# A two-layer hybrid attention block: the exponent's bias formed by ScalarE in layer 0 and by POOL in layer 1, with layer 1's bias tables spread over steps

## The chip, the core and the metric

One core of a Trainium2 chip runs the whole program. The metric is the device time of one execution in microseconds. The engines are TensorE (PE), VectorE (DVE), ScalarE (ACT), GpSimd (POOL) and SyncE (SP), which here only issues transfers; each works through its own queue in order, and they meet through semaphores. "L1536" is line 1536 of the kernel before.

## The reference

Two layers of a transformer block over 512 latent tokens and 256 context tokens of width 1024, one sample. Each layer: modulated RMS norm, one input projection, three groups of attention heads, output projection, gated residual, and a SwiGLU feed-forward part with its own norm and residual. Only layer 0 updates the context tokens.

```python
h = modulate(rms_norm(x, g_attn), sh_a, sc_a)
q_w, k_w, v_w, q_n, k_n, v_n, q_g, k_g, v_g = split_mixer_inputs(h @ w_in, qk_g)
o = concatenate([window_attention(...),         # A: 6 heads, window of 3 blocks, sink logits
                 neighbourhood_attention(...),  # B: 4 heads, 8 x 16 neighbourhood, position bias
                 global_block_attention(...)])  # C: 6 heads, all keys
x = x + ga_a * (o @ w_out)
x = x + ga_f * swiglu(modulate(rms_norm(x, g_ffn), sh_f, sc_f), w_gate, w_up, w_down)
# context queries (layer 0 only) attend to the 256 context keys alone
```

Every softmax is over local keys and the 256 context keys together. In each, the kernel computes the row maximum m of the scores, then exp(s * score - s * m + SHIFT), where s undoes a scale by a power of two that the queries and keys carry; so the bias of the exponent is (-s) * m + SHIFT.

## The kernel before

Attention is cut into steps (`STEPS`, index g): one head and 128 queries each. Layer 0 has 96: 24 of group A, 12 of context queries of A, 24 of group C, 20 of context queries of C and B, 16 of group B. Layer 1 has 64: 24 A, 24 C, 16 B. A step has 256 to 768 keys (768 in group C, 512 in B, 512 or 640 in A, 256 for context queries). Four steps make a group of one head (or two heads of context queries). The steps run from 234 to 446 us in layer 0 and from 1275 to 1425 us in layer 1; the rest of the time is projections and feed-forward, in which PE is the busy engine.

For step g, in order of dependence:

- `score(g)` on PE: scores into one of two PSUM buffers `acc[g % 2]` (L895, L896, masks L899). It waits for the exponent of step g-2.
- `top_of(g)` on DVE: in group B the bias table is added to the local scores (L1533), then `reduce_max` gives the row maximum into `stat` row 0 (L1536, semaphore `top`).
- `minus_top(g)` on DVE: the bias of the exponent, 128x1, into `stat` row 1 (L1543, semaphore `neg_top`).
- `softmax(g)` on ACT: the exponent of the scores with that bias and the sum of a row (L1199, an activation and the read of the accumulator; semaphore `exps`).
- `turn(g)` on PE: the probabilities are transposed, 128 columns at a time, into one of three banks (L912).
- `turned_high(g)` on ACT: the bank rounded to 16 bits, in pieces of up to 512 columns (L1221); `turned_low(g)` on DVE: the difference to it (L1550).
- `weigh(g)` on PE: both halves times the values (L927, L929) into `small`; after every fourth step `sum_outputs` on DVE adds the halves (L1558, L1562), and `take_output` on POOL divides by the row sums (L630, L632). `weigh` of the next group's first step waits for the sum.

Each engine has its order written out. DVE in iteration g: the sum of outputs if g is a multiple of four, `top_of(g)`, `minus_top(g)`, `turned_low(g-2)`. ACT: `turned_high(g-2)`, `softmax(g)`. PE: `score(g)`, `turn(g-2)`, `weigh(g-4)`, and in layer 0, every second or third step, a unit of modulation (`modulation`, L696 and L705), whose result ACT takes (L1210, L1213). The last three of the input projection's units (13 to 15) are finished within the first ten steps: norm (`norm_tile`, L1453 and L1464, which wait for a transfer of inverse norms), rounding (`round_high` L1157 on ACT, `round_low` L1491 on DVE) and eight transfers each, issued by SP.

POOL's main work is `split`: each tile of weights that a transfer has brought is rounded (L566) and its remainder formed (L569), two buffers deep. Its queue in the attention stage of layer 1 is: `split_next(0)` and `split_next(1)` for the first two tiles of the output weights, then for k in 0 to 15 `take_output(k)`, and after k = 8 to 11 one head's bias table (`bias_tables`: one scaling L606 and three additions L610). In layer 0 the splits of modulation weights lie between the outputs, and the tables follow k = 16 to 19. The remaining splits of output weights follow the last output.

## Time and profile before

| | |
|---|---|
| median of 3 runs (lowest, highest) | 1866.49 us (1864.91, 1866.91) |
| the profiled execution | 1864.14 us, its span 1862.3 us |
| PE, PEld busy | 1745.9 us (94%), 1475.2 us (79%) |
| DVE, ACT, POOL busy | 914.6 us (49%), 484.3 us (26%), 862.5 us (46%) |
| subtraction of the maximum, L1543 | 160 times, 34.3 us in all, 214 ns each |
| maximum, L1536 | 160 times, 117.4 us in all |
| exponent, L1199 | 160 times, 130.9 us, and 31.1 us of accumulator reads |
| idle time of ACT that L1543 ended | 55.0 us, 89 times |
| chain that ended last, share by engine | PE 79%, DVE 12%, issue 3%, DMA 2%, POOL 2%, ACT 2% |

The busy times are of the whole span, three quarters of which aren't attention. Within the two attention stages the shares are others, and they have to be read window by window. A row of the timeline gives the start in us, the length in us, engine, line, operation, output and input, and in brackets the idle time before it with what ended it. Instructions that don't depend on each other overlap a little at their ends: a row's length includes the time in which its result is written, while the next may have started.

### The profile page before, as it was taken

To read this page: it belongs to the slowest core of one execution; us is meant where nothing else is said; L and a number is where in the kernel's file an instruction comes from. 1 tells how busy PE (TensorE), PEld (TensorE's weight loads), DVE (VectorE), ACT (ScalarE), POOL (GpSimd) and SP (SyncE) were. 2 spreads that over 40 slices of the span, in tenths; PEclk is the share of its full clock that TensorE was granted. 3 is DMA by queue.
4 is the path that set the end of the run, shared out by engine and by line. 5 is a ranking of instruction groups with operands and counts; after the bars stand their busy time and mean duration, and the time that the engine had idled before them with its cause. 6 is when DMAs were issued, how large, how long until landed. Compare 5 with 4: busy or idle time off the path is not lost.

```text
span 1862.3 us, 30083 instructions
## 1 busy us (share of the span) xinstructions
PE 1745.9 (94%) x11175; PEld 1475.2 (79%) x11175; DVE 914.6 (49%) x1615; ACT 484.3 (26%) x984; POOL 862.5 (46%) x671
## 2 busy tenths in 40 slices
PE   5899979987989999999999998998887999999998
PEld 3588868976878888888888887887776778888886
DVE  2525478886355461255315455456996633123122
ACT  2212267775120100000000012224775121010010
POOL 0234337884324544444444453542021566666664
PEclk9999989999999999999999998998998999999999
DMA  8234444432114432334223322443200323333332
GB/s 293 46 91 115 114 120 120 132 92 57 57 38 132 124 102 68 102 114 122 80 80 112 116 65 46 113 110 100 50 2 1 91 79 94 98 92 100 92 94 96
DMA packets 316392, 174.42 MB, mean 94 GB/s; under 512 B 87550, under 2 KB 307598, under 8 KB 316302
## 3 DMA queue, kind: packets, MB, share of 16 engines
q1 hardware_dynamic: 288608, 148.54, 28.7%
q10 hardware_dynamic: 27694, 24.66, 4.2%
q8 instruction: 58, 0.95, 0.2%
q14 instruction: 32, 0.26, 0.0%
HBM read 159.04 MB, written 2.83 MB: 87 GB/s over the span
## 4 chain that ended last, share of the span: by engine, by line
PE 79%; DVE 12%; issue 3%; DMA 2%; POOL 2%; ACT 2%; SPq 1%; ACTq 0%; DVEq 0%; POOLq 0%
PE acc L746 66%; DVE prob_t L1550 3%; DVE stat L1536 3%; PE side L705 1%; PE mod_ps L818 1%; DVE o_sum L1562 1%; PE side L912 1%; PE small L988 1%; POOL split_w L569 1%; PE small L927 1%; PE acc L895 1%; PE acc L896 1%; PE mod_ps L716 1%; DVE stat L1543 1%; PE small L838 1%
## 5 line engine op out<-in xcount | busy, mean ns | idle before, releaser
L746 PE MATMUL acc<-act,split_w 128*128 128x512 f32 x5088 | 1006.3, 358 | 22.3 <-DVE act L1377 16.3
L746 PEld LDWEIGHTS acc<-act,split_w 128*128 128x128 f32 x5088 | 835.5, 190 | 171.6 <-issue 15.9
L569 POOL TENSOR_TENSOR split_w<-raw_w,split_w 128x1024 fp32r<-128x1024 f32 (+1 forms) x220 | 519.7, 2362 | 18.4
L566 POOL TENSOR_SCALAR split_w<-raw_w 128x1024 fp32r<-128x1024 f32 (+1 forms) x220 | 228.8, 1040 | 315.0 <-PE acc L746 205.2
L746 PE MATMUL acc<-hidden,split_w 128*128 128x512 f32 (+1 forms) x1584 | 308.8, 357 | 0.2 <-DVE hidden L1619 0.2
L746 PEld LDWEIGHTS acc<-hidden,split_w 128*128 128x128 f32 x1584 | 261.7, 188 | 46.0 <-DVE hidden L1619 0.6
L565 POOL TENSOR_TENSOR turnstile<-ones 128x1 f32<-128x1 f32 x136 | 53.6, 394 | 454.9 <-PE acc L746 454.9
L1617 DVE TENSOR_TENSOR prod<-acc,silu_g 128x768 f32<-128x768 f32 (+1 forms) x44 | 36.3, 824 | 331.1 <-PE acc L746 331.1
L1397 DVE SCALAR_TENSOR_TENSOR x_t<-acc,mod,x_t 128x512 f32 (+1 forms) x96 | 60.6, 659 | 258.4 <-PE acc L746 258.4
L1261 ACT ACTIVATE silu_g<-acc 128x768 f32<-128x768 f32 (+1 forms) x44 | 31.1, 706 | 455.3 <-PE acc L746 455.3
L1199 ACT ACTIVATE prob<-acc,stat,score_scale 128x768 f32<-128x768 f32 (+5 forms) x160 | 130.9, 818 | 57.1 <-DVE stat L1543 55.0
L1536 DVE TENSOR_REDUCE stat<-acc 128x1 f32<-128x768 f32 (+5 forms) x160 | 117.4, 734 | 22.8 <-PE acc L896 13.0
L1619 DVE TENSOR_TENSOR hidden<-prod,hidden 128x512 f32 (+2 forms) x44 | 105.3, 2392 | 45.7 <-ACT hidden L1269 45.7
L1642 DVE SCALAR_TENSOR_TENSOR mod_acc<-mod_chunk,silu_c,mod_acc 128x256 f32<-128x256 f32 x308 | 123.7, 473 | 0.0
L1269 ACT ACTIVATE hidden<-prod 128x512 f32 (+2 forms) x44 | 32.6, 740 | 314.9 <-DVE prod L1617 314.9
L927 PE MATMUL small<-v,prob_t 128*128 128x128 f16 x696 | 83.0, 223 | 26.6 <-DVE o_sum L1562 25.0
L895 PE MATMUL acc<-ks,qs 128*128 128x256 f16 (+1 forms) x384 | 94.8, 276 | 12.6 <-ACT prob L1199 12.1
L896 PE MATMUL acc<-ks,qs 128*128 128x256 f16 (+1 forms) x384 | 91.7, 274 | 0.0
L927 PEld LDWEIGHTS small<-v,prob_t 128*128 128x128 f16 x696 | 64.8, 100 | 33.2 <-DVE prob_t L1550 32.2
L630 POOL TENSOR_TENSOR o<-o_sum,stat 128x256 f32<-128x256 f32 x32 | 19.6, 612 | 146.7 <-DVE o_sum L1562 117.2
L912 PE MATMUL side<-ident,prob 128*128 128x128 f32 x470 | 79.2, 284 | 8.8 <-DVE prob_t L1550 8.4
L1550 DVE TENSOR_TENSOR prob_t<-side,prob_t 128x512 f16<-128x512 f32 (+2 forms) x154 | 84.2, 557 | 4.2 <-ACT prob_t L1221 2.5
(164 smaller groups left out, 1568.2 us busy)
## 6 DMA issues: line engine op xcount, KB each, us to landing
raw_w<-in_w_gate SPq DMA_DIRECT2D x44, 512.0 KB, 3.9
raw_w<-in_w_up SPq DMA_DIRECT2D x44, 512.0 KB, 3.8
mod_chunk<-in_w_mod ACTq DMA_DIRECT2D x22, 1024.0 KB, 5.3
raw_w<-in_w_mod SPq DMA_DIRECT2D x36, 512.0 KB, 3.9
raw_w<-in_w_in SPq DMA_DIRECT2D x64, 256.0 KB, 3.7
raw_w<-in_w_down SPq DMA_DIRECT2D x32, 512.0 KB, 4.0
mod_start<-in_w_mod SPq DMA_DIRECT2D x4, 2048.0 KB, 12.6
ks<-q_split SPq DMA_DIRECT2D x64, 96.0 KB, 2.2
```

The lines of the kernel that those rows point to most:

```text
L566: pool.tensor_scalar(split_w[slot][:, 0, 0:n, :], raw_w[slot][:, 0:n, :], 1.0, 0.0, ALU.mult, ALU.add).then_inc(hi_w, 1)
L569: pool.tensor_tensor(split_w[slot][:, 1, 0:n, :], raw_w[slot][:, 0:n, :], split_w[slot][:, 0, 0:n, :].bitcast(F32), ALU.subtract).then_inc ...
L746: mm = pe.matmul(acc[slot][:, a:b], split_w[slot][:, part == 2, k, :], moving[:, part == 1, k, a:b], start=(k == 0 and part == 0), stop=(k ...
L895: pe.matmul(out_, q, ks[:, s["k"], 0, k0:k0 + size], start=True, stop=False)
L896: mm = pe.matmul(out_, q, ks[:, s["k"], 1, k0:k0 + size], start=False, stop=not masks)
L912: mm = pe.transpose(turned_at[BANK_AT["p", c] % 3][:, t - a:t - a + P], prob[g % 3][:, 1 + t:1 + t + P], ident[:, :])
L927: pe.matmul(small[:, at_:at_ + 128], prob_t[g % 4][:, 0, P * t:P * t + P], v[:, 2 * vc:2 * vc + 128], start=(t == 0), stop=False)
L1199: sc.activation(prob[g % 3][:, 1 - s["sink"]:1 + n], src, ACT.Exp, bias=stat[:, 1, i:i + 1], scale=score_scale[:, 0, gi:gi + 1], accum_out ...
L1536: ve.reduce_max(stat[:, 0, i:i + 1], src, AX_X).then_inc(top, 1)
L1550: ve.tensor_tensor(prob_t[g % 4][:, 1, a:b], turned_at[BANK_AT["p", c] % 3][:, 0:b - a], prob_t[g % 4][:, 0, a:b], ALU.subtract).then_inc( ...
L1619: ve.tensor_tensor(hidden[:, 1, bass.ds(f, 1), 0:w].rearrange("p a t -> p (a t)"), prod[0][:, 0:w], hidden[:, 0, bass.ds(f, 1), 0:w].rearr ...
L1642: i = ve.scalar_tensor_tensor(**kw, in1=mod_acc[:, b, :], op0=ALU.mult, op1=ALU.add)
```

## The change

`minus_top` is removed from DVE. In layer 0, ACT forms the bias itself: at the start of `softmax(g)` it waits for the maximum, runs an Identity activation of 128x1 with a scale from `score_scale` and a bias from the new constant `exp_shift`, waits for its own result and then runs the exponent. In layer 1, POOL does it with the same `tensor_scalar` as DVE did. POOL's queue in layer 1 becomes a loop over steps: the subtraction of step i; from i = 11 every fourth step the output of group (i - 11) / 4; and in steps 30 to 45 one operation of the bias tables each (scaling, or one of three additions), where before a table's four came together. The two splits of output weights stay ahead of that loop. POOL's order in layer 0 is unchanged.

```diff
+        exp_shift = place("exp_shift", [P, 1], F32)
...
+            pool.memset(exp_shift[:, :], SHIFT).then_inc(filled, 1)
...
-                def bias_tables(h):
-                    if l == 0 and h == 0:
-                        pool.wait_ge(consts_in, N_CONST * 16)
-                    if h == 0:
+                def bias_tables(h, i):
+
+                    if h == 0 and i == 0:
+                        if l == 0:
+                            pool.wait_ge(consts_in, N_CONST * 16)
                         pool.wait_ge(wide_in, 16 * 4 * ROWS * (l + 1))
                         pool.wait_ge(unit_done, u_in(l) + 16)
...
+                def minus_top(g):
+
+                    s, i = STEPS[g], g - LAYER_STEPS[l][0]
+                    gi = 3 * l + "ABC".index(s["group"])
+                    pool.wait_ge(top, g + 1)
+                    pool.tensor_scalar(stat[:, 1, i:i + 1], stat[:, 0, i:i + 1], score_scale[:, 2, gi:gi + 1], SHIFT, ALU.mult,
+                                       ALU.add).then_inc(neg_top, 1)
...
-                for k in range(N_GROUPS[l]):
+                for k in range(N_GROUPS[l] if l == 0 else 0):
...
-                    if (16 if l == 0 else 8) <= k < (20 if l == 0 else 12):
-                        bias_tables(k - (16 if l == 0 else 8))
+                    if 16 <= k < 20:
+                        for i in range(4):
+                            bias_tables(k - 16, i)
+                for i in range(4 * N_GROUPS[l] + 8 if l else 0):
+                    if i < 4 * N_GROUPS[l]:
+                        minus_top(LAYER_STEPS[l][0] + i)
+                    if i >= 11 and i % 4 == 3:
+                        take_output((i - 11) // 4)
+                    if 30 <= i < 46:
+                        bias_tables((i - 30) // 4, (i - 30) % 4)
...
                 def softmax(g):
                     s = STEPS[g]
                     i, n, gi = g - LAYER_STEPS[l][0], s["n"], 3 * l + "ABC".index(s["group"])
+                    if l == 0:
+                        if g == 0:
+                            sc.wait_ge(filled, 3)
+                        sc.wait_ge(top, g + 1)
+                        sc.activation(stat[:, 1, i:i + 1], stat[:, 0, i:i + 1], ACT.Identity, bias=exp_shift[:, 0:1],
+                                      scale=score_scale[:, 2, gi:gi + 1]).then_inc(neg_top, 1)
                     sc.wait_ge(neg_top, g + 1)
...
-                def minus_top(g):
-
-                    s, i = STEPS[g], g - LAYER_STEPS[l][0]
-                    gi = 3 * l + "ABC".index(s["group"])
-                    ve.wait_ge(top, g + 1)
-                    ve.tensor_scalar(stat[:, 1, i:i + 1], stat[:, 0, i:i + 1], score_scale[:, 2, gi:gi + 1], SHIFT, ALU.mult,
-                                     ALU.add).then_inc(neg_top, 1)
-
...
                         top_of(g)
-                        minus_top(g)
```

## Rows read from the trace of the kernel before

**Rows 1.** Busy time by windows: us, PE, PEld, DVE, ACT, POOL, PEclk, DMA

```profile
330.00:390.00 60.00, 58.07 (x769) 54.29 (x768) 49.38 (x107) 46.75 (x120) 48.63 (x33) 1.00 0.44 127
...
1345.00:1384.00 39.00, 36.17 (x426) 30.43 (x422) 38.36 (x81) 32.79 (x71) 7.82 (x12) 1.00 0.01 2
```

**Rows 2.** Timeline of DVE, layer 1, group C: one group of four steps

```profile
1358.11 0.95 DVE L1536 TENSOR_REDUCE stat<-acc 128x1 f32<-128x768 f32 x1
...
1359.23 1.01 DVE L1550 TENSOR_TENSOR prob_t<-side,prob_t 128x512 f16<-128x512 f32 x2
1360.16 0.95 DVE L1536 TENSOR_REDUCE stat<-acc 128x1 f32<-128x768 f32 x1
...
1366.36 0.66 DVE L1562 TENSOR_REDUCE o_sum<-small 128x256 f32<-128x512 f32 x1
1366.94 0.95 DVE L1536 TENSOR_REDUCE stat<-acc 128x1 f32<-128x768 f32 x1
```

**Rows 3.** Timeline of ACT, layer 1, group C, the same steps

```profile
1361.39 0.99 ACT L1199 ACTIVATE prob<-acc,stat,score_scale 128x768 f32<-128x768 f32 x1 [0.20 <-DVE stat L1543]
...
1362.38 0.58 ACT L1221 ACTIVATE prob_t<-side 128x512 f16<-128x512 f32 x1
```

**Rows 4.** POOL: an output in the timeline, and two lines' lengths (min/median/max)

```profile
1367.10 0.61 POOL L630 TENSOR_TENSOR o<-o_sum,stat 128x256 f32<-128x256 f32 x1 [8.21 <-DVE o_sum L1562]
...
L565 POOL TENSOR_TENSOR turnstile<-ones x136: 192/194/2693, 520.9 to 1844.0; 128x1 f32<-128x1 f32 x136
...
L606 POOL TENSOR_SCALAR wide<-wide,score_scale x8: 579/586/589, 399.4 to 1394.3; 128x384 f32<-128x384 f32 x8
```

**Rows 5.** Timeline of DVE and ACT, layer 1, group B

```profile
1402.58 0.69 DVE L1536 TENSOR_REDUCE stat<-acc 128x1 f32<-128x512 f32 x1
...
1404.49 0.69 DVE L1536 TENSOR_REDUCE stat<-acc 128x1 f32<-128x512 f32 x1
...
1410.89 0.69 DVE L1536 TENSOR_REDUCE stat<-acc 128x1 f32<-128x512 f32 x1
...
1405.47 0.78 ACT L1199 ACTIVATE prob<-acc,stat,score_scale 128x512 f32<-128x512 f32 x1 [0.55 <-DVE stat L1543]
```

**Rows 6.** Timeline of DVE, layer 1, group A: the maxima of steps 13 and 16

```profile
1311.08 0.83 DVE L1536 TENSOR_REDUCE stat<-acc 128x1 f32<-128x641 f32 x1
...
1316.91 0.69 DVE L1536 TENSOR_REDUCE stat<-acc 128x1 f32<-128x513 f32 x1
```

**Rows 7.** Timeline of POOL, ACT and DVE at the start of attention in layer 1

```profile
1281.81 2.35 POOL L569 TENSOR_TENSOR split_w<-raw_w,split_w 128x1024 fp32r<-128x1024 f32 x1
...
1279.18 0.78 ACT L1199 ACTIVATE prob<-acc,stat,score_scale 128x513 f32<-128x513 f32 x1
...
1281.61 0.83 DVE L1536 TENSOR_REDUCE stat<-acc 128x1 f32<-128x641 f32 x1 [0.78 <-PE acc L899]
...
1284.05 0.48 DVE L1453 SCALAR_TENSOR_TENSOR q_raw<-raw_q,vecs,root 128x256 f32<-128x256 f32 x1 [1.37 <-DMA root<-inv_rows]
...
1285.91 0.69 DVE L1550 TENSOR_TENSOR prob_t<-side,prob_t 128x512 f16<-128x512 f32 x1
```

**Rows 8.** ACT's Identity of two columns, lengths (min/median/max)

```profile
L1210 ACT ACTIVATE mod<-side,vecs x26: 250/262/278, 263.8 to 432.9; 128x2 f32<-128x2 f32 x26
```

**Rows 9.** Timeline of ACT and DVE, layer 0, context queries: one group

```profile
394.67 0.57 ACT L1199 ACTIVATE prob<-acc,stat,score_scale 128x256 f32<-128x256 f32 x1
...
396.67 0.57 ACT L1199 ACTIVATE prob<-acc,stat,score_scale 128x256 f32<-128x256 f32 x1
...
399.33 0.57 ACT L1199 ACTIVATE prob<-acc,stat,score_scale 128x256 f32<-128x256 f32 x1 [0.71 <-DVE stat L1543]
...
398.63 0.41 DVE L1536 TENSOR_REDUCE stat<-acc 128x1 f32<-128x256 f32 x1
```

**Rows 10.** Timeline of POOL at the start of layer 1's attention

```profile
1275.09 1.04 POOL L566 TENSOR_SCALAR split_w<-raw_w 128x1024 fp32r<-128x1024 f32 x1 [11.16 <-DMA raw_w<-in_w_out]
...
1279.92 1.80 POOL L566 TENSOR_SCALAR split_w<-raw_w 128x1024 fp32r<-128x1024 f32 x1 [1.36 <-DMA raw_w<-in_w_out]
```

## What the change is predicted to do

> **What bounds the kernel now.** I read the windows first, then the timeline inside them, then the chain of waits in order of time. The change touches only the two attention stages (234 to 446 us in layer 0, 1275 to 1425 us in layer 1). In layer 1, DVE is busy 38.36 of 39.00 us while PE has 36.17, ACT 32.79 and POOL 7.82; in the corresponding part of layer 0, where PE also computes modulations, it is PE that is full (58.07 of 60.00 us) and DVE has 49.38 [rows 1]. So one operation removed from DVE can shorten layer 1 and the parts of layer 0 where PE is not the last; where PE is, it buys nothing.
>
> The timeline of DVE shows what the subtraction costs there. In group C a step is 2.04 us (maximum to maximum). The maximum that starts at 1358.11 ends at 1359.06, and the first difference of the turned probabilities starts at 1359.23; the subtraction lies in that gap of 0.17 [rows 2]. The next maximum begins at 1360.16, 0.08 before the two differences end (1360.24): independent instructions of DVE overlap by that much. Without the subtraction the difference could start at 1358.98, so the slot is worth 0.25 us; I take 0.23, since the overlap behind a reduction is not shown. Four steps and one sum of outputs make a group of 1366.94 - 1358.11 = 8.83 us [rows 2].
>
> **What takes the subtraction's place in layer 1.** Now the way from the end of the maximum to the exponent is x = 0.28 us (maximum of 1360.16, which ends at 1361.11, to the exponent at 1361.39) [rows 2, 3]. With POOL there are two handoffs. DVE to POOL is 0.08 us: the sum of outputs ends at 1367.02, POOL starts at 1367.10 [rows 2, 4]. To ACT I take 0.04. The subtraction itself, 128x1 on POOL, isn't shown: its nearest rows are the turnstile's product, also 128x1, 0.194 us in the median, and the scaling of 384 columns with a pointer, 0.586 [rows 4]. It is nearest to the first; with a little for the pointer I take 0.23, and x = 0.35. The ends are x = 0.31 and 0.71.
>
> This matters because the next limit is near. ACT turns the older tile high only after the exponent of the step before, and DVE's difference waits for that. From one maximum to the one two steps on: 0.95 (maximum) + x + 0.99 (exponent 1361.39 to turned-high 1362.38) + 0.61 (turned-high and handoff) + 0.93 (two differences, 1359.23 to 1360.16) = 3.48 + x [rows 2, 3]. Twice that with the sum's 0.66 is a group: 7.62 + 2x. Now it is 8.18, hidden under DVE's 8.83. Afterwards DVE alone would need 8.83 - 4 x 0.23 = 7.91, and the loop, 8.32, is the later one. **Group C gains 0.51 us, not 0.92; six groups, 3.1 us.**
>
> Group B has a step of 1.91 and a group of 8.31 us (1402.58 to 1410.89) [rows 5]. Its loop is 0.69 (maximum) + x + 0.78 (exponent) + 0.61 + 1.05 (what a step of 1.91 leaves beside the maximum and the gap of 0.17: the difference and the addition of the bias) = 3.13 + x; the group 6.92 + 2x = 7.62, DVE alone 7.39 [rows 5, 2]. **Gain 0.69, four groups, 2.8 us.**
>
> Group A already waits on the way round through PE: from the maximum at 1311.08, over its exponent, the scores two steps later, the turn and both halves of the split, to the maximum at 1316.91, three steps; only one step of four is DVE alone [rows 6]. So a group gains 0.23 and pays x - 0.28 = 0.07: 0.16, for three settled groups 0.5 us.
>
> **The start of layer 1 pays.** POOL's queue has the splits of the first two tiles of the output weights ahead of the first subtraction, and the second of them ends at 1284.16. The exponent of step 0 started at 1279.18 [rows 7]. Behind the waiting POOL instruction stand all further subtractions; behind them ACT's exponents, PE's scores of step 2 (they reuse the bank) and then DVE. Step by step: subtraction 0 ends at 1284.35, exponent 0 with its accumulator read at 1285.3; the scores of step 2 and their handoff take 1.5 us, as now (exponent and read end at 1280.1, maximum 2 starts at 1281.61), so it starts near 1286.8; then come the two operations of unit 13 (from 1284.05 now, where they waited for a transfer), and the first difference falls at about 1289.45 instead of 1285.91 [rows 7]. That is 3.5 us late, not 5.2, because 1.6 us of it were spent waiting for the transfer. The slots removed up to step 11 give back little over 0.4 of it, since split and exponent are then waited for: **+3.1 us**. The transfer of unit 15, 2 us later, still lands before it is read.
>
> The bias tables in layer 1 become one operation a step (0.59 or 0.74 us) in steps 30 to 45. Before, four in a row would have held up a subtraction for 2.8 us; now at most 0.74 + 0.61 (the output) lie between two that are 1.9 us apart, so I cost them at nothing. If that cover failed, 0.1 us a step, 1.6 in all. The outputs are taken three steps later, well before their buffer is wanted two groups on. The loads of the bias lie ahead of step 30 in the timeline, so POOL doesn't wait for them there.
>
> Layer 1: 3.1 - 0.5 - 3.1 - 2.8 = -3.3; as a function of the handoff, 25x - 12.0 us.
>
> **Layer 0, with ACT.** An Identity with a bias takes 0.262 us [rows 8]; from the maximum's end to the exponent y = 0.03 + 0.25 + 0.04 = 0.32. Exponent and Identity exist side by side there already without table loads between them. Four parts:
> - Context queries (32 steps, 8 groups). From exponent to exponent: two steps of 2.00 together (394.67 to 396.67), then 1.96 to the next group's maximum and 0.70 to its exponent, 4.66 in all (to 399.33) [rows 9]. ACT's step becomes 0.56 (exponent, read) + 0.27 + 0.29 (Identity, which the exponent must wait for) = 1.12 instead of 1.00: 2.24 + 1.96 + 0.73 = 4.93. **+0.27 a group, +2.2 us.** The bounds: 0 and 0.29 in every one of 32 steps, 9 us, which would need ACT to be last everywhere; it isn't at the sum.
> - Group C (24 steps): PE is full there [rows 1]. ACT's step would be 0.99 + 0.86 (two turned-high) - 0.1 (overlap) + 0.29 = 2.04, under the 2.6 us at which PE runs on average with a modulation in every second step: +0.3, from 0 to 2.
> - Group B: as in layer 1 with y: 7.56 against 8.31, 0.75; in one of four groups a modulation on PE is last: -2.3.
> - Start: DVE is on the chain up to the load that follows unit 15; five slots of 0.2, less 0.28 for the Identity before the first exponent: -0.7. Group A behind it waits for weights and PE: 0.
>
> Layer 0: -0.5. **Sum: -3.8 us.** It is made against the profiled execution (span 1862.3, 1864.14 with what lies around it); the median of the runs is 1866.49, 2.35 above that, and the difference is applied to it: 1862.7.
>
> **Port.** At 1279.92 POOL's scaling of 1024 columns took 1.80 us, beside DVE's difference of unit 12, which has both inputs in SBUF; at 1275.09, alone, the same form took 1.04 [rows 10]. The Trainium skill (SBUF — State Buffer, two separate sides) says the two engines share one port pair as an exclusive lock, for DVE instructions with two SBUF inputs, and that the loser is blocked for the whole instruction. By that rule a form of 1.04 is held for 0.76 us here; the trace agrees. The maxima and differences of the steady part read PSUM, and POOL's product at 1367.10, beside a maximum, took its usual 0.61 [rows 4]. Only seven operations of units 12 to 15, in steps 1 to 9, remain, and most of what they delay waits for PE anyway.
>
> **Rivals.**
> 1. DVE alone sets the pace (a slot saved is a slot won, the loop is shorter than I add up). C 5.5, B 3.7, A 2.8 won in layer 1, +3.1 at the start, -0.5 in layer 0: -9.4 us, 1857.1. For it: DVE 98% busy [rows 1]. Against it: the loop adds up from rows and is over DVE's need. Chance 0.15.
> 2. The handoff over POOL is long. From x = 0.48 layer 1 gains nothing, from x = 0.65 (0.53 us on POOL) the kernel is slower by over 3.7; at the upper end, 0.71, it is +5.7 in layer 1, +5.2 in all: 1871.7. For it: the 384 columns' 0.586; against it: the median of the 128x1 product. Chance 0.12.
> 3. The lock of the port holds the subtractions of steps 2 to 9 and each hold reaches the end: 4 x 0.76 beside the differences and 3 x 1.86 beside the norms (1284.05 to 1285.91) [rows 7] = 8.6 us on top of the forecast, 1871.3. Chance 0.07; against it, ACT and PE have 0.5 to 2 us of slack in six of the seven places.
> 4. No change: x near 0.5 (0.38 on POOL), or ACT in layer 0 costs 3 us more: 1866. Chance 0.24.
> The forecast has 0.42.
>
> **How the numbers follow.** A kernel of this time is told from no change at about 0.2%, 3.7 us. The forecast sits on that bound, so half of it counts as faster (0.21) and half as same; with rival 1, and a little of rival 4, faster is 0.37; same 0.44; rivals 2 and 3, slower, 0.19. The range from 1858 to 1870.5 takes in the forecast and rival 4, and of the others the milder halves.
>
> **What would show it.** Right: POOL's new row near 0.23 us, 64 times; group C of layer 1 near 8.3 us, B near 7.6, DVE idle behind ACT's turned-high; the first exponent of layer 1 at about 1284 (less what layer 0 won); a group of context steps near 4.9. Wrong: groups of C at 7.9 (rival 1) or 8.8 and more (2); POOL rows of 1 us in steps 2 to 9 with idle DVE behind them (3); a table load between Identity and exponent in each step would end the whole sum.

## The result, and the profile after

The changed kernel takes 1870.87 us in the median of 10 runs (1867.29 to 1873.18), the kernel before, run in turns with it, 1866.33 (1862.42 to 1870.43): ratio 1.0026, 95% interval 1.0015 to 1.0037. It is slower by 0.26%, where 0.2% gain was forecast. The profiled execution took 1871.29 us, its span is 1869.5, 7.2 us over that of before.

The two new kinds of instruction first: all subtractions on POOL (L624) and all Identities on ScalarE (L1219) of the changed kernel. Columns: count, length in ns (min/median/max), first and last start, shapes.

```profile
L624 POOL TENSOR_SCALAR stat<-stat,score_scale x64: 267/267/1322, 1288.1 to 1417.9; 128x1 f32<-128x1 f32 x64
...
L1219 ACT ACTIVATE stat<-stat,exp_shift,score_scale x96: 371/386/394, 242.3 to 450.0; 128x1 f32<-128x1 f32 x96
```

POOL's takes 0.267 us, near the 0.23 assumed; ScalarE's takes 0.386, where the row of an Identity that was used as its price has 0.262 [rows 8]. The windows of the changed kernel that answer to [rows 1] (us, then busy PE, PEld, DVE, ACT, POOL, granted clock, share and GB/s of the transfers):

```profile
330.00:390.00 60.00, 58.75 (x767) 54.87 (x767) 46.02 (x79) 53.12 (x141) 49.11 (x33) 1.00 0.44 126
1345.00:1384.00 39.00, 35.77 (x449) 32.08 (x448) 37.12 (x65) 33.60 (x76) 18.34 (x38) 1.00 0.01 2
```

In layer 1 DVE is no longer full (37.12 of 39.00 against 38.36) although more steps fit in; in layer 0 ScalarE has become much busier (53.12 of 60 against 46.75).

To see where time went, I compared the starts of all 160 maxima, before and after. d is after minus before:

| place | before, us | d |
|---|---|---|
| layer 0, step 0 | 234.37 | +3.82 |
| step 24, context queries of A begin | 301.92 | +3.50 |
| step 36, group C begins | 318.93 | +6.42 |
| step 60, context queries of C and B begin | 382.32 | +6.98 |
| step 80, group B begins | 410.45 | +8.83 |
| step 95, the last | 441.41 | +7.88 |
| layer 1, step 0 | 1275.74 | +4.89 |
| step 12 | 1309.23 | +6.04 |
| step 24, group C begins | 1332.07 | +5.36 |
| step 48, group B begins | 1385.06 | +3.13 |
| the last step, 63 | 1416.88 | +0.20 |
| feed-forward of layer 1, the long chain begins | 1499.80 | +2.05 |
| the end of the span | 1862.3 | +7.2 |

Layer 0's attention loses 4.1 us (3.82 to 7.88) and layer 1's gains 4.7 (4.89 to 0.20). But 7.0 us appear behind both, in stages whose instructions the change doesn't touch, 5.2 of them from the start of the long chain on, and 3.0 are won between the two attention stages. The first 3.8 stand there before the change acts; the runs below show such an offset between -3.9 and +3.8 at step 0, one per execution, and I leave it out of everything. The late loss is in one row of the chain of work that ended last (start, length, line, number of matmuls), of before and of after:

```profile
1499.80 318.90 PE acc L746 x1392
```

```profile
1501.85 323.74 PE acc L766 x1392
```

The same 1392 matmuls of 512 columns, back to back, at a granted clock of 1.00 in both: 229.1 ns each before, 232.6 ns after. In layer 0's feed-forward the opposite holds: 480 matmuls take 84.88 us before and 84.38 after. Something in the change altered the pace of TensorE where no instruction of it was changed. The one thing in the diff that reaches so far is the new tile: `exp_shift` takes 64 bytes in the layout, and every tile placed behind it (the activations `act`, `hidden`, the queries, keys and values) starts 64 bytes later.

### The profile page after: what moved, and what is told of

Same layout as the page of the kernel before. It is cut to its first block, busy times and chain, and to the rows that moved or that the text cites. A ratio compares the mean times of both kernels' runs of the same rounds, so it can differ in the third digit from the quotient of the medians.

```text
span 1869.5 us, 30085 instructions
## 1 busy us (share of the span) xinstructions
PE 1749.2 (94%) x11175; PEld 1475.4 (79%) x11175; DVE 887.9 (47%) x1455; ACT 512.1 (27%) x1080; POOL 884.3 (47%) x736
## 4 chain that ended last, share of the span: by engine, by line
PE 79%; DVE 7%; issue 4%; ACT 4%; POOL 2%; DMA 2%; SPq 1%; ACTq 0%; DVEq 0%; POOLq 0%
PE acc L766 65%; ACT prob_t L1247 1%; PE side L932 1%; PE mod_ps L838 1%; DVE prob_t L1568 1%; DVE stat L1562 1%; PE small L947 1%; PE acc L915 1%; POOL split_w L571 1%; PE side L725 1%; PE acc L916 1%; ACT prob L1225 1%; DVE o_sum L1580 1%; PE small L1008 1%; PE mod_ps L736 1%
## 5 line engine op out<-in xcount | busy, mean ns | idle before, releaser
L949 PE MATMUL small<-v,prob_t 128*128 128x64 f16 x696 | 77.9, 195 | 0.0
```

## The experiments

Theory P: the loss is that place effect, ScalarE's work in layer 0 costs less than 2 us, and POOL's part in layer 1 does what was predicted. Rival Q: the attention stages alone account for the loss, and the pace of the matmuls is chance.

### 1. Only the room: e1_room_only

```diff
         eps = place("eps", [P, 1], F32)
+        room = place("room", [P, 1], F32)
```

> The kernel before, with one unused tile of 64 bytes placed behind eps, where the change places its new tile exp_shift; every tile behind it (act, hidden, the queries, keys and values among them) moves by 64 bytes, and no instruction is added, removed or reordered. Theory P (place): the change's own loss lies in TensorE's streams outside attention, whose matmuls of 512 columns took 232.6 ns with the change against 229.1 before (1392 of them, +4.8 us, and +0.7 in two shorter chains), those of 384 columns 176.7 against 177.5 (-3 us in all); then this kernel is 2 to 5 us slower than before, about +0.2%, and shows 232 to 233 ns in the long chain of layer 1. Theory Q (attention): the loss lies in layer 0's attention, which the profiled pair shows 4.1 us longer, and the rate of the matmuls is a matter of the execution: then this kernel is within 1 us of before and shows 229 ns, or either rate at random.

Measured: 1867.04 us (12 runs) against 1864.69, ratio 1.0018, interval 1.0008 to 1.0027; the long chain takes 323.75 us, 232.6 ns a matmul, and the 480 of layer 0 84.38 us, what the changed kernel shows, to 0.01 us. By the ratio an unused tile of 64 bytes costs 3.4 us, with an interval from 1.5 to 5.0; the medians lie 2.4 us apart, and the trace of this kernel is 3.1 us longer than that of before, counted from the first maximum. On the place, P holds.

### 2. The whole change, nothing moved: e2_same_addresses

```diff
+        eps_at = at[0]
         eps = place("eps", [P, 1], F32)
-        exp_shift = place("exp_shift", [P, 1], F32)
+        exp_shift = place("exp_shift", [P, 1], F32, eps_at + 32)
```

> The whole change, but exp_shift placed in the unused 32 bytes behind eps, so that no other tile moves. Theory P: the long chain of layer 1 goes back to 229 ns a matmul and the kernel is 2 to 5 us faster than the changed kernel, 1866 to 1869, at most 0.1% from before. Theory Q: as the changed kernel, +0.2 to +0.3% against before.

Measured: 1866.79 us against 1864.69, ratio 1.0007 (0.9996 to 1.0017); the chain is back at 318.90 us. The edit itself isn't told from no change. The two ratios differ by 0.19%, with an uncertainty of some 0.15%: most of the 0.26% came from where a constant was put.

### 3. POOL in layer 1 alone: e3_pool_only

The diff of the change without exp_shift and without ScalarE's part; in layer 0 VectorE subtracts:

```diff
                         top_of(g)
+                        if l == 0:
+                            minus_top(g)
```

> POOL subtracts in layer 1, with the bias tables spread over steps; layer 0 as before on VectorE, no exp_shift, all addresses as before. The prediction's terms for layer 1 sum to -3.3 us; the profiled pair shows -4.7 for that stage (start +1.15, groups of A -0.22, of C -0.39, of B -0.55 to -0.7 each). Theories P and Q: 3 to 5 us faster than before, ratio 0.997 to 0.9985. If instead the gain of a shorter attention stage is given back behind it (the same total at another place), the ratio is 0.9995 to 1.0005 and the stretch from the last step to the end is longer by as much.

Measured: 1861.31 us (12 runs) against 1864.69, ratio 0.9985 (0.9976 to 0.9995). Layer 0's maxima lie at -0.18 to -0.33 us against before at every step, so nothing disturbs the reading. In layer 1 d goes from +0.32 at step 0 to +2.32 at step 12 (start: +2.0), to +1.62 at step 24 (A: -0.7), to -0.68 at step 48 (C: -2.3), to -3.63 at the last (B: -2.95): -3.95 in all.

### 4. ScalarE in layer 0 alone: e4_act_only

```diff
+                    if l == 0:
+                        if g == 0:
+                            sc.wait_ge(filled, 3)
+                        sc.wait_ge(top, g + 1)
+                        sc.activation(stat[:, 1, i:i + 1], stat[:, 0, i:i + 1], ACT.Identity, bias=exp_shift[:, 0:1],
+                                      scale=score_scale[:, 2, gi:gi + 1]).then_inc(neg_top, 1)
                     sc.wait_ge(neg_top, g + 1)
...
-                        minus_top(g)
+                        if l:
+                            minus_top(g)
```

> ScalarE forms the bias in layer 0, layer 1 as before, exp_shift in the gap behind eps, all addresses as before. The prediction's terms for layer 0 sum to -0.5 us (context steps +2.2, C +0.3, B -2.3, start -0.7). Theory P: within 2 us of before (the 4.1 of the profiled pair hold a stretch of 7 us at a granted clock of 0.6 to 0.7, at 315 to 322 us, that is not the change's). Theory Q: 3 to 6 us slower, ratio 1.0015 to 1.003, with the context groups at 5.2 us and more where 4.93 was forecast, and group B at 8.1 where 7.56 was.

Measured: 1869.84 us against 1864.69, ratio 1.0027 (1.0019 to 1.0036). Here P's figure (within 2 us) is missed and Q's is hit, in the context groups and group B too (5.30 and 8.06 us): ScalarE's part costs 5 us by itself. Both effects are real: place +0.18%, ScalarE +0.27%, POOL -0.15% add to +0.30% beside the 0.26% of the whole change; each of the three is known to about 0.1%, so that they agree this closely is in part luck. The profiled execution, whose trace is read here, was with 1873.79 us the second slowest of 11. d in layer 0: step 0 +2.23, step 24 +0.41, step 36 +3.31, step 60 +3.84, step 80 +7.77, step 95 +6.80.

What a context step has become shows in ScalarE's timeline of this kernel (start, length, line, operation, in brackets the idle time before it):

```profile
400.40 0.56 ACT L1208 ACTIVATE prob<-acc,stat,score_scale 128x256 f32<-128x256 f32 x1
400.86 0.19 ACT L1208 ACTIVATION_READ_ACCUMULATOR prob<-acc,stat,score_scale 128x1 f32 x1
400.95 0.37 ACT L1230 ACTIVATE prob_t<-side 128x256 f16<-128x256 f32 x1
...
401.22 0.38 ACT L1202 ACTIVATE stat<-stat,exp_shift,score_scale 128x1 f32<-128x1 f32 x1
401.63 0.57 ACT L1208 ACTIVATE prob<-acc,stat,score_scale 128x256 f32<-128x256 f32 x1
```

No idle time: ScalarE is full, and from exponent to exponent it is 1.23 us, where 1.12 was predicted and 1.00 was before [rows 9]. The Identity is followed by the exponent only at 401.63, 0.41 after its own start.

And a second thing, in the windows of e4_act_only:

```profile
310.00:325.00 15.00, 12.46 (x114) 10.56 (x113) 8.62 (x24) 11.76 (x38) 8.69 (x7) 0.77 0.33 89
...
410.00:420.00 10.00, 9.25 (x79) 8.01 (x80) 5.89 (x16) 6.71 (x21) 9.19 (x12) 0.66 0.28 80
```

The granted clock is 0.77 and 0.66 in these two, in or behind context queries: part of each was run at 1.2 GHz instead of 2.4. In the kernel before the first of them stands at 1.00:

```profile
310.00:325.00 15.00, 12.44 (x147) 10.87 (x145) 12.68 (x36) 11.32 (x34) 11.04 (x9) 1.00 0.29 79
```

Ahead of the second one TensorE had idled more, 6.34 us busy in 10 us against 7.53 before; experiment 9 has a trace that speaks against this as the whole cause. The changed kernel has the first fall as well (0.77) and not the second: its groups of context steps from step 76 to 80 take 6.19 us, those of e4_act_only 8.27. So one fall costs 2.1 us. e2_same_addresses, the whole change, has both falls (0.77, and 0.68 in the second window).

### 5. The context steps back on VectorE: e6_context_on_vector

```diff
-                    if l == 0:
+                    if l == 0 and s["local"]:
...
-                        if l:
+                        if l or not STEPS[g]["local"]:
                             minus_top(g)
```

(ScalarE's own steps count on a semaphore of their own.)

> ScalarE forms the bias in the local steps of layer 0 only; in its 32 context steps, and in layer 1, VectorE subtracts as before; a semaphore of its own orders ScalarE's part; addresses as before. Theory K (context steps): in e4_act_only ScalarE is full in them, a step takes 1.235 us instead of 1.00, and TensorE, which then idles, falls to half its clock at 315 and at 410 us; without them the granted clock stays at 1.00 there, the stage keeps the gains of groups A and B (-1.8 and -0.95 us) and the kernel is 1 to 3 us faster than before, ratio 0.9985 to 0.9995. Theory L (the drop of the clock is set off by group A's altered rhythm or by group C's): a stretch at 0.5 to 0.6 near 315 us remains, and the kernel is at least 1 us slower than before.

Measured: 1865.86 us (11 runs) against 1865.81, ratio 1.0001 (0.9992 to 1.0010). Neither theory's time came: K had 1 to 3 us less than before, L at least 1 us more. The clock, as K had it, stays at full speed in both places,

```profile
310.00:325.00 15.00, 12.44 (x147) 10.95 (x148) 11.65 (x36) 11.13 (x36) 10.14 (x9) 1.00 0.29 78
...
410.00:420.00 10.00, 8.47 (x96) 7.26 (x94) 9.17 (x23) 8.44 (x24) 9.75 (x11) 1.00 0.30 86
```

and the context groups are back at their old length (d is +2.05 at step 24 and +1.90 at step 36, +2.33 at step 64 and +2.32 at step 80). Against e4_act_only, 0.26% is won back: it is the context steps that cost ScalarE's part its time. But the kernel is not faster than before: its trace gains 0.9 us in layer 0, and group A, which gained 1.8 us in e4_act_only, gains 0.2 here. In e4_act_only and in the changed kernel the clock is full from 270 to 290 us; here, as in the kernel before, it is 0.91. Up to the end of group A ScalarE does the same in these two kernels, and yet one trace has this fall and the other hasn't. I can say where the falls stood, not what places them.

### 6. The cost of the Identity: e12_copy_without_shift

```diff
-                        sc.activation(stat[:, 1, i:i + 1], stat[:, 0, i:i + 1], ACT.Identity, bias=exp_shift[:, 0:1],
+                        sc.activation(stat[:, 1, i:i + 1], stat[:, 0, i:i + 1], ACT.Copy,
                                       scale=score_scale[:, 2, gi:gi + 1]).then_inc(neg_top, 1)
```

> e4_act_only with ScalarE's Identity replaced by a Copy that takes the scale from its tile and no bias: the constant SHIFT is left out of the exponent in layer 0 (it cancels in the quotient but for rounding). The Identity with two operands from tiles measured 0.386 us where the prediction took 0.262, the row of an Identity with one. If the second operand makes that difference, the Copy takes 0.25 to 0.27, a context step 1.11 us instead of 1.235, and groups of context steps fall from 5.1 to 5.3 us to the 4.9 that was predicted. If the length has another reason (one column, source in SBUF), it stays at 0.38 and nothing moves.

```profile
L1202 ACT ACTIVATE stat<-stat,score_scale x96: 278/295/302, 237.1 to 440.4; 128x1 f32<-128x1 f32 x96
```

0.295 us instead of 0.386, 0.091 less. The edit takes away the bias operand and also puts Copy for Identity, and no run separates the two; but [rows 8] is an Identity with one operand from a tile and takes 0.262, which points to the second operand. The Trainium skill (ScalarE: Activation LUTs, What ACT_TABLE_LOAD costs) gives about 93 ns for each operand of scale or bias that is a column of a tile, on top of 186 ns with immediates. An estimate by that page is 0.28 us with one and 0.37 with two; the trace agrees to 0.02 us.

Over 96 steps that takes 8.7 us of work from ScalarE. The one execution took 1864.24 us, 0.7 under the median of before on its chip, where e4_act_only was 5.2 over its own. From the first to the last maximum of layer 0 its trace is 6.1 us shorter than that of e4_act_only; the two falls of the clock, which it doesn't have, are 4.2 of them. d in layer 0: step 0 -0.17, step 24 -2.13, step 36 -1.78, step 60 -1.53, step 80 -0.33, step 95 -1.71. The two context groups from step 64 take 5.04 and 5.13 us instead of 5.30 and 5.33 (4.93 was predicted). The clock doesn't fall in either place (it does at the stage's end, from about 442 us on, without a visible price); from step 33 to step 40 d grows by 0.66 us, in the changed kernel by 2.72, which gives a fall's cost a second time, 2.1 us:

```profile
310.00:325.00 15.00, 12.69 (x145) 11.14 (x146) 10.49 (x24) 12.87 (x43) 10.56 (x9) 1.00 0.35 96
...
410.00:420.00 10.00, 9.53 (x119) 8.62 (x118) 9.33 (x19) 8.38 (x24) 9.75 (x10) 1.00 0.22 62
```

With the price that the prediction had assumed, nearly, layer 0 comes out at -1.5 us (-0.5 predicted). It is one execution; the steps inside it are as steady as in the others, the total is not to be read to a microsecond.

### 7. The start of layer 1: e5_vector_first_ten

```diff
-                    if i < 4 * N_GROUPS[l]:
+                    if 10 <= i < 4 * N_GROUPS[l]:
                         minus_top(LAYER_STEPS[l][0] + i)
...
-                        if l == 0:
+                        if l == 0 or g - g0 < 10:
                             minus_top(g)
```

> POOL in layer 1 alone, as in e3_pool_only, but the subtractions of the first ten steps stay on VectorE, so that none waits behind POOL's two splits and none meets VectorE's operations with two SBUF inputs. Theory S (the start costs what the prediction said): in e3_pool_only the maximum of step 12 is 2.0 us later against before than that of step 0; here it is level to within 0.4 us, and the kernel is 2 us faster than e3_pool_only: 5 to 6 us faster than before, ratio 0.9965 to 0.9975. Theory T (the lateness is made up later in any case, since what follows waits for the last units and weights): the time of e3_pool_only, ratio 0.998 to 0.999.

Measured: 1859.20 us (5 runs) against 1865.81, ratio 0.9965 (0.9951 to 0.9978). d goes from -2.21 at step 0 to -2.79 at step 12 and to -8.65 at the last step: 6.4 us won in the stage instead of 3.95. S holds: the first twelve steps win 0.6 where they lost 2.0, and what the start costs is not made up later.

### 8. What the place does: e7_room_128, e8_room_192, e11_weights_moved_too

As experiment 1, with 32 and 48 columns instead of one; in e11_weights_moved_too a tile of 64 bytes stands ahead of all tiles, the weights included. e7, e8 and e11 were run once each.

> The kernel before with 128 unused bytes behind eps. act, hidden and what follows then begin 64 bytes past a multiple of 256, where before they begin 192 past one and with 64 bytes added at one. Theory U (bits of the address above 64 bytes decide the rate): a third pair of rates, neither 229.1 and 176.8 ns nor 232.6 and 175.8, or the first pair again if only whether the address is a multiple of 128 counts. Theory V (any tile moved against the weights does it): the pair 232.6 and 175.8.

> As e7_room_128 with 192 bytes: act begins 128 past a multiple of 256. If only a multiple of 128 counts: 232.6 ns in layer 1 and 175.8 in layer 0, as with 64 bytes added. If 256 counts: 229 and another rate in layer 0.

> The kernel before with 64 unused bytes ahead of all tiles: the weights (split_w) move with act and hidden. If the address of the streamed tile alone decides, act begins at a multiple of 256 again and the rates are those of e1_room_only, 232.6 and 175.8 ns. If the distance between the weights and the streamed tile decides, it is unchanged and the rates are those of before, 229.1 and 176.8. Any other pair: both addresses take part.

| `act` moved against the weights | kernels | 1392 matmuls of layer 1, us | ns each | 480 of layer 0, us |
|---|---|---|---|---|
| 0 bytes | before, e2, e3, e4, e5, e6, e12 | 318.90 to 318.91 | 229.1 | 84.88 to 84.91 (e5: not in its chain) |
| 0, all moved by 64 | e11 | 318.90 | 229.1 | see below |
| 64 bytes | the change, e1 | 323.74, 323.75 | 232.6 | 84.38 |
| 128 bytes | e7 | 325.08 | 233.5 | 84.90 |
| 192 bytes | e8, e9, e10 | 315.82 to 315.84 | 226.9 | 83.31 (e8, e10) |

The rows of the chain for e8_room_192 and e11_weights_moved_too:

```profile
1491.26 315.82 PE acc L747 x1392
```

```profile
1498.30 318.90 PE acc L747 x1392
```

(e11's chain doesn't run through the 480 of layer 0; in the 220 us from 760 on it has 1272 matmuls, as the kernel before.) The pace of layer 1's chain repeats within a layout to 0.02 us in 320, over 14 executions on several chips, so it belongs to the layout, not to the execution. U holds for layer 1: there are four paces in steps of 64 bytes, and V falls. For 192 bytes 232.6 or 229 ns were expected, and neither came. e11 shows that the address of the streamed tile alone isn't what counts: with `split_w` moved along, the pace is the old one. The distance between tiles counts; that the weights are the other end of it is likely, but `x_t` and `raw_w` moved with them, so it is not shown. The Trainium skill (TensorE: Matmul & The Clock Gate, Step-by-step: what each phase is for) says that the streamed operand and the weights have read ports of their own, and that loading weights takes no bandwidth from a running matmul. No run here tests that statement; what they show is that the places of the tiles matter all the same, by up to 2.9% of a matmul.

e8_room_192 took 1852.24 us in its one run, 13.6 under the median of before; e7_room_128 took 1875.84.

### 9. The parts together: e10_change_and_room, e9_first_ten_and_room

The first is the whole change with 128 more bytes behind `exp_shift`; the second is experiment 7 with 192 bytes behind `eps`.

> The whole change with 128 unused bytes behind exp_shift, so that act, hidden and the rest lie 192 bytes further than before, as in e8_room_192, and not 64. Theory A: the change alone at unmoved addresses was +0.07%, and the place is worth what e8_room_192 shows: 1853 to 1856 us, ratio 0.993 to 0.995; the same edit, placed otherwise, is faster than the kernel before by ten times what its own work is worth. Against it: the rates go back to those of the changed kernel (232.6 and 175.8 ns), since exp_shift itself is what disturbs; then 1869 to 1872.

> e5_vector_first_ten (POOL subtracts from step 10 of layer 1 on, VectorE everywhere else) with 192 unused bytes behind eps. Theory A (the place of the tiles and the work in attention add up): e5_vector_first_ten was 6.5 us under before, and e8_room_192, one run, 13 to 14 us; the sum gives 1845 to 1847 us, ratio 0.989 to 0.990, with 227 ns in layer 1's long chain and 173.6 in layer 0's. Theory B (e8_room_192's single run was partly luck in the first 70 us, where executions differ by up to 8 us): the rates are the same, but the time is 1848 to 1853, ratio 0.991 to 0.993.

Measured: e10_change_and_room 1859.07 us (1846.38 to 1861.48, 7 runs) against 1864.95, ratio 0.9962 (0.9946 to 0.9979). The same edit that lost 0.26% wins 0.38% with one unused tile behind its constant. Both expected times, 1853 to 1856 and 1869 to 1872, were missed. e9_first_ten_and_room 1853.58 (1842.92 to 1856.79, 6 runs), ratio 0.9925 (0.9903 to 0.9947): it is 11 us under the kernel before, but less than the sum of its parts would give (theory B's ratio). Why shows in the windows of layer 0's feed-forward, first e8_room_192, then e9_first_ten_and_room:

```profile
760.00:980.00 220.00, 220.00 (x1296) 193.38 (x1295) 90.56 (x179) 14.13 (x17) 101.66 (x76) 1.00 0.34 104
```

```profile
760.00:980.00 220.00, 220.00 (x1270) 191.69 (x1270) 84.54 (x168) 14.10 (x17) 98.87 (x75) 1.00 0.34 103
```

1296 matmuls against 1270 in the same 220 us, from the same addresses, both at full clock and without a pause. From the last maximum of layer 0 to the first of layer 1, e9 is 8.0 us slower than e8. e10's profiled execution, the fastest of its seven, has 1297 matmuls there. So at this layout three traces show two paces in layer 0. That an execution gets one or the other fits the wide spread of these two kernels (15.1 and 13.9 us), but each was traced once, so it isn't shown. B had looked for the cause in the first 70 us; it is here. What chooses the level wasn't tried.

e10_change_and_room says something on the clock too. It is the whole change, with Identities of 0.386 us, and its clock stays full from 270 to 445 us. The 10 us ahead of the first fall, first e4_act_only, then e10:

```profile
304.00:314.00 10.00, 6.90 (x80) 5.62 (x80) 6.65 (x20) 8.98 (x29) 8.21 (x7) 1.00 0.44 117
```

```profile
304.00:314.00 10.00, 6.91 (x80) 5.62 (x80) 6.66 (x20) 8.99 (x29) 7.62 (x6) 1.00 0.44 117
...
310.00:325.00 15.00, 11.67 (x135) 10.14 (x134) 10.55 (x26) 12.99 (x41) 10.61 (x8) 1.00 0.33 87
...
410.00:420.00 10.00, 8.46 (x104) 7.49 (x101) 7.97 (x18) 8.81 (x27) 9.75 (x12) 1.00 0.35 101
```

TensorE and ScalarE did the same work at the same time, and the clock fell in one trace and not in the other. So neither the Identity's length nor TensorE's idle time decides alone whether a fall comes: the whole change has one fall in its own trace, two in e2_same_addresses and none here. The four traces with the full Identity in the context steps have five falls near 315 and 410 us; the ten others, e12_copy_without_shift among them, have none there. The comparison of e10 with the changed kernel gives a fall's price with the instructions unchanged: steps 32 to 36 take 5.60 us against 7.64.

## Why the prediction was wrong, step by step

**The step that was missing: where the new tile lies.** The prediction went through every instruction of the diff and gave its first line, the place of `exp_shift`, no term at all. It is worth +3.4 us (e1_room_only), two thirds of the loss, and lies almost wholly in stages that the prediction set aside as untouched. In the trace of e1_room_only it is +4.85 in the long chain, +0.4 behind it, +1.0 between layer 1's attention and the chain, and -2.4 between the two attention stages.

**Layer 0, the Identity: a term mis-sized.** The price was taken from a row with one operand from a tile; this one has two: 0.386 us instead of 0.262. The way from maximum to exponent, y, is 0.45 instead of 0.32 (in e4_act_only the maximum of 425.88 ends at 426.57, its exponent starts at 427.02). A context group is then, by the prediction's own sum, 2 x 1.235 + 1.96 + 0.41 + 0.45 = 5.29; measured are 5.30 and 5.33, not 4.93. The sum was right and the figure put into it wrong. The context steps as a whole come near the forecast all the same, which is luck, since groups with modulations pay less: +0.8 from step 24 to 36 and +1.8 from step 60 to 80, 2.6 in all for the +2.2 forecast, once the two falls of the clock are taken off.

**Layer 0, group B.** -0.75 a group was predicted, -0.13 to -0.27 came in a whole group; -0.97 in all instead of -2.3. The loop sum gives 6.92 + 2 x 0.45 = 7.82 for a group, and in three steps of four it wasn't the last limit: ScalarE was, which the prediction had not added up for this group. Its rows in e4_act_only have no idle time from 426.60 to 433.9:

```profile
427.02 0.78 ACT L1208 ACTIVATE prob<-acc,stat,score_scale 128x512 f32<-128x512 f32 x1
427.70 0.19 ACT L1208 ACTIVATION_READ_ACCUMULATOR prob<-acc,stat,score_scale 128x1 f32 x1
427.79 0.59 ACT L1230 ACTIVATE prob_t<-mod_ps 128x512 f16<-128x512 f32 x1
428.27 0.39 ACT L1202 ACTIVATE stat<-stat,exp_shift,score_scale 128x1 f32<-128x1 f32 x1
428.69 0.78 ACT L1208 ACTIVATE prob<-acc,stat,score_scale 128x512 f32<-128x512 f32 x1
...
429.46 0.25 ACT L1219 ACTIVATE mod<-side,vecs 128x2 f32<-128x2 f32 x1
429.60 0.25 ACT L1222 ACTIVATE mod_row<-side 4x128 f32<-4x128 f32 x1
...
430.83 0.78 ACT L1208 ACTIVATE prob<-acc,stat,score_scale 128x512 f32<-128x512 f32 x1
...
434.67 0.39 ACT L1202 ACTIVATE stat<-stat,exp_shift,score_scale 128x1 f32<-128x1 f32 x1 [0.74 <-DVE stat L1545]
```

A step takes 1.67 us, the next 2.14 with a modulation's two small operations, then 1.74. The fourth takes 2.52: there ScalarE waits 0.74 for the maximum, which stands behind VectorE's difference and sum of outputs. Together 8.07.

**Layer 0, the clock: a mechanism that was missing.** No step and no rival had it. With ScalarE full in the context steps, TensorE's clock falls to 1.2 GHz once (the changed kernel), twice (e4_act_only, e2_same_addresses) or not at all (e10_change_and_room), 2.1 us each time; against it one fall near 280 us is gone, which is most of what group A gained in e4_act_only. That the mis-sized Identity is at the root of the falls is not shown: in the one execution of e12_copy_without_shift, 0.09 us less an instruction, neither comes, but neither comes in e10_change_and_room either, with the full length. What the medians show is that the context steps on ScalarE cost 0.26% (e6_context_on_vector against e4_act_only); how that divides between full ScalarE and clock over many executions is open. Of the 5.1 us between forecast (-0.5) and trace (+4.6) of e4_act_only, the two falls are 4.2, group B 1.3, the context steps 0.4, group C 0.2, less 1.1 that the start and group A did better. Rival 4 ("ACT in layer 0 costs 3 us more") named the place and neither size nor mechanism.

**Layer 1: right in its mechanism, the sum in part by luck.** The forecast was -3.3 us, e3_pool_only shows -3.95 in its trace and -3.4 in its median. By terms the trace has +2.0 at the start (forecast +3.1), -0.7 in group A (-0.5), -2.3 in group C (-3.1) and -2.95 in group B (-2.8): a start that was forecast too dear and a group C that was forecast too good cancel. The way from the maximum to the exponent, x, and the loop that it closes can be read in group C of the changed kernel:

```profile
1362.40 0.95 DVE L1562 TENSOR_REDUCE stat<-acc 128x1 f32<-128x768 f32 x1
...
1370.85 0.95 DVE L1562 TENSOR_REDUCE stat<-acc 128x1 f32<-128x768 f32 x1
...
1363.45 0.27 POOL L624 TENSOR_SCALAR stat<-stat,score_scale 128x1 f32<-128x1 f32 x1 [1.11 <-DVE stat L1562]
...
1363.75 1.00 ACT L1225 ACTIVATE prob<-acc,stat,score_scale 128x768 f32<-128x768 f32 x1 [0.91 <-POOL stat L624]
...
1365.35 0.69 DVE L1568 TENSOR_TENSOR prob_t<-mod_ps,prob_t 128x512 f16<-128x512 f32 x1 [0.21 <-ACT prob_t L1247]
```

The maximum ends at 1363.35, POOL starts 0.10 later, the exponent at 1363.75: x = 0.40 (0.35 assumed; between the bounds 0.31 and 0.71). The formula 7.62 + 2x gives 8.42; the group measures 8.45. The 0.05 us more of x take 0.1 of the 0.51 forecast for a group. In group B it gives 6.92 + 0.80 = 7.72; e3_pool_only has 7.73:

```profile
1400.31 0.69 DVE L1554 TENSOR_REDUCE stat<-acc 128x1 f32<-128x512 f32 x1
...
1408.04 0.69 DVE L1554 TENSOR_REDUCE stat<-acc 128x1 f32<-128x512 f32 x1
```

VectorE, which rival 1 held to be alone on the path, waits for ScalarE's turned-high (the 0.21 in brackets above); rival 1 is out. Rival 2 is out with POOL's 0.267. Group A gained 0.23 a group, where 0.16 was forecast.

**The start of layer 1: right in kind, a third too dear.** In the changed kernel:

```profile
1285.06 2.92 POOL L571 TENSOR_TENSOR split_w<-raw_w,split_w 128x1024 fp32r<-128x1024 f32 x1
1288.08 0.63 POOL L624 TENSOR_SCALAR stat<-stat,score_scale 128x1 f32<-128x1 f32 x2
...
1288.38 0.78 ACT L1225 ACTIVATE prob<-acc,stat,score_scale 128x513 f32<-128x513 f32 x1 [4.32 <-POOL stat L624]
...
1290.80 0.83 DVE L1562 TENSOR_REDUCE stat<-acc 128x1 f32<-128x641 f32 x1 [5.02 <-PE acc L919]
```

The first subtraction waits for the second split, ScalarE for it 4.32 us, VectorE 5.02. In e3_pool_only the maximum of step 2 falls at 1287.39 (1286.8 predicted) and the lateness at step 12 is 2.0 us, not 3.1: more was made up on the way than the 0.4 allowed.

**The port: the mechanism right, no price, as forecast.** In e3_pool_only POOL's subtraction is held by VectorE's operations with two SBUF inputs:

```profile
1297.25 1.34 DVE L1482 SCALAR_TENSOR_TENSOR q_raw<-raw_q,vecs,inv 128x512 f32<-128x512 f32 x1
...
1299.95 1.32 DVE L1482 SCALAR_TENSOR_TENSOR q_raw<-raw_q,vecs,root 128x512 f32<-128x512 f32 x1
...
1297.43 1.31 POOL L622 TENSOR_SCALAR stat<-stat,score_scale 128x1 f32<-128x1 f32 x1 [1.06 <-DVE stat L1554]
...
1300.12 1.29 POOL L622 TENSOR_SCALAR stat<-stat,score_scale 128x1 f32<-128x1 f32 x1 [1.38 <-DVE stat L1554]
```

Two of 1.3 us and, at 1303.85 and 1306.18, two of 0.64 instead of 0.27. Yet the lateness falls all the while, from 4.09 at step 3 to 2.32 at step 12. Rival 3's 8.6 us didn't come. My reading, not tried apart: the differences that need the held exponent stand behind the same VectorE operation that holds it, so both are late together. The spread of the bias tables cost nothing: the steps with a table operation on POOL (group C) follow the formula.

**The bookkeeping.** Forecast -3.8: layer 1 -3.3, layer 0 -0.5. By the runs alone: layer 1 -0.15%, layer 0 +0.27%, place +0.18%, together +0.30%; the change measured +0.26%. The place alone doesn't explain the miss: with no tile moved (e2_same_addresses) the change measures +0.07%, from -0.04 to +0.17, where -0.20% was forecast; what is left is ScalarE's part in layer 0.

## What to carry to other kernels

A new constant is an edit of the memory layout: place it in a gap, or compare the rows of a stage that the change doesn't touch before believing any verdict of some tenths of a per cent; and where TensorE streams all day, try the layouts, since the place of one tile moved this kernel further than the edit did. Price a small instruction by a row with the same number of operands from tiles, and when work goes from one engine to another, add up the receiving engine step by step for every kind of step, small extras included. TensorE's clock can fall for some microseconds in a stage that leaves it idle time, and in another kernel with the same instructions in that stage it may not; no sum of instructions shows it, and a single trace doesn't tell what a change did to it.

## What the runs showed of the hardware that was not expected

- The pace of back-to-back matmuls in layer 1's long chain depends on the distance of the streamed tile from the tiles ahead of it: 226.9, 229.1, 232.6 and 233.5 ns for 512 columns at 192, 0, 64 and 128 bytes added, the same in all 14 traces.
- Layer 0's matmuls (512 and 256 columns in turn) follow another order: 83.31 us for 480 at 192 bytes, 84.38 at 64, 84.9 at 0 and 128; at 192 bytes one of three traces ran at the slower level.
- A bias from a tile beside a scale from a tile costs ScalarE 0.091 us, even on one column (measured with Copy against Identity).
- POOL's subtraction on 128x1, with an operand from a tile, takes 0.267 us; beside a VectorE operation with two SBUF inputs it took up to 1.32.
- One fall of TensorE's clock in the context steps costs 2.1 us, and where the falls come differs between traces: near 280 us in some, at 315 and 410 in others, and in none of these places in e10_change_and_room, though TensorE and ScalarE did the same there as in e4_act_only ahead of 315.
